# Two norms behind gated residuals: their shift seeded into PSUM by TensorE, residual and sums of squares by halves of the columns, shift vectors summed as columns

## The chip, the cores and the metric

The kernel runs on one core of a Trainium2 chip. The metric is the device time of one execution in microseconds. The kernel before took 904.48 us (median of three runs, 904.3 to 905.38).

## The reference, cut to what matters

The input is 256 tokens of 1024 features in float32. A first block (attention, then a squared-ReLU MLP) is followed by two modulated layers. Each modulated layer makes six vectors of 1024 from a condition `c`, and uses them as shift, scale and gate:

```python
def ada_modulation(c, ada_w, ada_b):
    m = jax.nn.silu(c) @ ada_w + ada_b
    return jnp.split(m, N_MOD, axis=-1)          # sh_m, sc_m, g_m, sh_f, sc_f, g_f

def modulate(h, shift, scale):
    return h * (1.0 + scale[:, None, :]) + shift[:, None, :]

def odd_layer(x, c, ...):
    h = modulate(rms_norm_2(x, mix_norm), sh_m, sc_m)
    ...                                          # qkv, stick-breaking attention
    x = x + g_m[:, None, :] * (o @ w_out)
    hf = modulate(rms_norm_2(x, ffn_norm), sh_f, sc_f)
    return x + g_f[:, None, :] * swiglu(hf, ffn_w_gate, ffn_w_up, ffn_w_down)
```

The layer before it (`even_layer`) has the same form, with a convolution and a linear recurrence in place of attention. The change touches the two norms of the odd layer: the one in front of its qkv projection (behind layer 0's swiglu and its gate `g_f`), and the one in front of its swiglu (behind the output projection and the gate `g_m`).

## The kernel before, in words

The 256 tokens lie as two tiles of 128 on the partitions (tile 0, tile 1), with 1024 columns each. `x` is the residual, `xn` the normed rows. TensorE needs the normed rows transposed, so they are transposed in blocks of 128 x 128 into two PSUM banks per tile (`norm_T`), and are copied from there to `aT_hi` by ScalarE (`norm_hi`), with the rest after rounding in `aT_lo` by VectorE (`norm_lo`). Every product is made of three matmuls in the rounded type fp32r: hi x hi, hi x lo, lo x hi.

Weights stream through four slots of 128 x 1024 elements ("parts"). SyncE's queue loads part v into `w_raw`, ScalarE rounds it to `w_hi` (L691), VectorE makes `w_lo` (L1104), TensorE uses both and then counts `w_used`. ScalarE may not write a slot before TensorE has counted `w_used` for the part three before it; SyncE may not load one before VectorE has made the `w_lo` of the part four before it. A unit is two parts. All engines run their instructions strictly in the order written; in the attention-like stages this order is written out by hand in the strings `ATT_STEPS`, `LRU_STEPS` and `STICK_STEPS` (H: round a part to `w_hi`, L: its `w_lo`, U and P: products of a unit or a part, and so on). Each engine picks from the string the steps that are its own.

The order of stages that matters here: the LRU stage (layer 0, mixer), ending with the output projection, units U10 to U13; the entry of layer 0's swiglu (`entry(U_SG0)`, norm number k = 3); the swiglu loop; the entry of the qkv stage (`entry(U_QKV2)`, k = 4); the stick stage (layer 1, attention, and its output projection P24 to P30); the entry of layer 1's swiglu (`entry(U_SG1)`, k = 5); the swiglu loop and the last residual. The three entries are called the **first**, the **second** and the **third entry** below.

An entry works like this. TensorE ends the products of the stage before, tile 0 first (`tile0_done`), then tile 1 (`w_used`). VectorE multiplies tile 0 by the gate and adds it to `x` (`gate`, `add_gated`: L1223, L1227), ScalarE squares and sums the row (L701), GpSimd makes 1/sqrt of the mean (L613, L614), VectorE has meanwhile multiplied `x` by the gain (`norm_scale`, L1118) and then makes `xn * rstd + shift` in two halves of 512 columns (`norm_rows`, L1127). TensorE transposes (L1831), ScalarE copies the banks (L744), and products with the first unit's weights follow (L1876, in `entry`): six groups for tile 0 with `aT_hi`, of which the last two want `w_hi` of parts 2 and 3 of that entry, then two with `aT_lo`, then the transposes of tile 1, and so on. At the second and third entry ScalarE's program rounds parts 2 and 3 in between (`norm`, L719 to L738). Norms k = 1 and 2 already work by halves of the columns and take their 1/sqrt from ScalarE's Ln and Exp (`half_square`, `half_rstd`: L714, L708, L710).

The modulation vectors are accumulated by VectorE as products per partition (`ada`), so each is spread over 128 partitions and has still to be summed over them. `ada_sums` (L2034 to L2042) does that with a matmul of `ones` (128 x 128, float32) and 512 columns of the vector, which gives the sum on every partition; ScalarE copies it back from PSUM (`ada_parts`, L747 to L755). Twelve such matmuls belong to layer 1: four at the first entry, four behind layer 0's swiglu at the second, four in front of layer 1's swiglu at the third. `ada_gain` (L1313) makes (1 + scale) x gain of the sum.

ScalarE's functions come in table sets; Silu, Sigmoid and Ln with Exp are in different ones, Copy and Square in all. Before, one set is loaded at the start of the stick stage (L1044), another in front of its Sigmoids (L1059).

## Time and profile before

| what | value |
|---|---|
| median of three runs | 904.48 us |
| the profiled execution's own time | 904.1 us |
| its span in the trace | 901.9 us |
| TensorE busy | 890.9 us (99%), 5057 matmuls |
| VectorE busy | 691.2 us (77%) |
| ScalarE busy | 486.3 us (54%) |
| granted TensorE clock, mean | 0.999 |
| chain that ended last | TensorE 94%, VectorE 2%, ScalarE 2%, DMA 1%, issue 1% |

The profile is one execution; its own time is that of the span and 2.2 us around it. A timeline row gives the start in us from the span's start, the length in us, the engine (PE is TensorE, PEld its loads of the stationary operand, DVE VectorE, ACT ScalarE, POOL GpSimd), the line, the operation, out and in with shapes, the count, and in brackets how long the engine was idle before and what ended that. The lengths of matmuls include their pipeline, so starts, not ends, tell how fast they follow one another. A float32 matmul stands in the trace as two matmuls with a load each; an fp32r matmul and a transpose as one.

### The profile page before, as it was taken

What the parts mean: (1) busy time and instruction counts of PE and PEld (TensorE: products, weight loads), DVE (VectorE), ACT (ScalarE), POOL (GpSimd) and SP (SyncE); (2) the same over time, 40 slices, a digit from 0 to 9 for tenths busy, and PEclk for the clock granted to TensorE, in tenths of its full rate; (3) what the DMA queues carried; (4) which work ended last, traced back from release to release, by engine and by line L of the source; (5) the groups of instructions that cost most, each with busy time, mean ns of one, the idle gap of its engine ahead of it and who ended that gap; (6) DMA issues with size and microseconds to landing.
All of it is one profiled execution on the core that took longest, in us unless ns stands there. A gap on an engine that the chain in (4) does not pass through costs nothing.

```text
span 901.9 us, 13646 instructions
## 1 busy us (share of the span) xinstructions
PE 890.9 (99%) x5057; PEld 762.2 (85%) x5057; DVE 691.2 (77%) x719; ACT 486.3 (54%) x650; POOL 29.4 (3%) x52
## 2 busy tenths in 40 slices
PE   8999999999999999999999999999999999999998
PEld 5998879999999799879888888878777888888886
DVE  4698978988888885976888888687797775555655
ACT  5545574444445657755454455455674465545542
POOL 4000100000000000012000000010000100000000
PEclk9999999999999999999999999999999999999999
DMA  6989586999998385645988888626434366656561
GB/s 217 339 273 341 177 292 215 356 362 328 321 329 311 107 269 162 213 139 171 370 304 315 321 302 286 190 90 217 139 117 139 107 209 198 189 186 186 187 188 68
DMA packets 117093, 208.08 MB, mean 231 GB/s; under 512 B 7236, under 2 KB 81068, under 8 KB 111928
## 3 DMA queue, kind: packets, MB, share of 16 engines
q1 hardware_dynamic: 116566, 205.31, 67.5%
q10 hardware_dynamic: 290, 2.10, 0.7%
q8 instruction: 30, 0.49, 0.2%
q14 instruction: 15, 0.12, 0.0%
q0 software_dynamic: 192, 0.05, 0.0%
HBM read 206.39 MB, written 1.05 MB: 230 GB/s over the span
## 4 chain that ended last, share of the span: by engine, by line
PE 94%; DVE 2%; ACT 2%; DMA 1%; issue 1%; SPq 0%; DVEq 0%; ACTq 0%
PE tp L1858 8%; PE ub L1858 8%; PE acc L1763 7%; PE acc L1764 7%; PE acc L1766 7%; PE acc L1711 5%; PE acc L1713 5%; PE acc L1712 5%; PE tp L1859 4%; PE ub L1859 4%; PE acc L1876 4%; PE tp L1876 4%; PE ub L1847 3%; PE ub L1846 3%; PE ub L1845 3%; PE acc L1845 2%
## 5 line engine op out<-in xcount | busy, mean ns | idle before, releaser
L1104 DVE TENSOR_TENSOR w_lo<-w_raw,w_hi 128x1024 fp32r<-128x1024 f32 x288 | 348.6, 1221 | 117.3 <-ACT w_hi L691 116.7
L691 ACT ACTIVATE w_hi<-w_raw 128x1024 fp32r<-128x1024 f32 x288 | 302.2, 1058 | 245.2 <-PE acc L1766 72.4
L1858 PE MATMUL tp<-aT,w_hi 128*128 128x512 f32 x320 | 114.1, 399 | 0.0
L1858 PE MATMUL ub<-aT,w_hi 128*128 128x512 f32 x320 | 113.8, 398 | 0.0
L1763 PE MATMUL acc<-w_hi,hT_hi 128*128 128x512 f32 x288 | 112.8, 392 | 0.1
L1764 PE MATMUL acc<-w_lo,hT_hi 128*128 128x512 f32 x288 | 112.2, 390 | 0.0
L1766 PE MATMUL acc<-w_hi,hT_lo 128*128 128x512 f32 x272 | 106.1, 390 | 0.0
L1859 PE MATMUL tp<-aT,w_lo 128*128 128x256 f32 x320 | 89.9, 281 | 0.0
L1859 PE MATMUL ub<-aT,w_lo 128*128 128x256 f32 x320 | 89.8, 281 | 0.0
L1858 PEld LDWEIGHTS tp<-aT,w_hi 128*128 128x128 f32 x320 | 60.1, 188 | 14.9
L1858 PEld LDWEIGHTS ub<-aT,w_hi 128*128 128x128 f32 x320 | 60.1, 188 | 14.6
L1845 PE MATMUL ub<-aT,w_hi 128*128 128x256 f32 x256 | 72.5, 283 | 0.0
L1846 PE MATMUL ub<-aT,w_hi 128*128 128x256 f32 x256 | 72.4, 283 | 0.0
L1847 PE MATMUL ub<-aT,w_lo 128*128 128x256 f32 x256 | 72.4, 283 | 0.0
L1711 PE MATMUL acc<-w_hi,aT 128*128 128x512 f32 x168 | 67.5, 402 | 0.2 <-DVE aT L1112 0.2
L1713 PE MATMUL acc<-w_hi,aT 128*128 128x512 f32 x168 | 65.5, 390 | 0.0
L1712 PE MATMUL acc<-w_lo,aT 128*128 128x512 f32 x168 | 65.5, 390 | 0.0
L1763 PEld LDWEIGHTS acc<-w_hi,hT_hi 128*128 128x128 f32 x288 | 54.1, 188 | 11.6 <-issue 0.3
L1764 PEld LDWEIGHTS acc<-w_lo,hT_hi 128*128 128x128 f32 x288 | 54.1, 188 | 10.5
L1859 PEld LDWEIGHTS ub<-aT,w_lo 128*128 128x128 f32 x320 | 60.4, 189 | 0.7
L1766 PEld LDWEIGHTS acc<-w_hi,hT_lo 128*128 128x128 f32 x272 | 51.1, 188 | 11.3
L1859 PEld LDWEIGHTS tp<-aT,w_lo 128*128 128x128 f32 x320 | 60.4, 189 | 0.0
(274 smaller groups left out, 1524.2 us busy)
## 6 DMA issues: line engine op xcount, KB each, us to landing
ada_raw<-in_l_ada_w SPq DMA_DIRECT2D x24, 1024.0 KB, 6.2
w_raw<-in_l_ffn_w_gate SPq DMA_DIRECT2D x44, 512.0 KB, 4.5
w_raw<-in_l_ffn_w_up SPq DMA_DIRECT2D x44, 512.0 KB, 3.9
w_raw<-in_l_ffn_w_down SPq DMA_DIRECT2D x44, 512.0 KB, 3.4
w_raw<-in_w_up SPq DMA_DIRECT2D x32, 512.0 KB, 4.4
w_raw<-in_w_down SPq DMA_DIRECT2D x32, 512.0 KB, 5.1
scratch<-in_l_ada_w SPq DMA_DIRECT2D x14, 1024.0 KB, 7.3
w_raw<-in_attn_w_qkv SPq DMA_DIRECT2D x24, 512.0 KB, 6.2
```

Of the source, the lines that this page charges most:

```text
L691: act.activation(w_hi[:, v % SLOTS, :], w_raw[:, v % SLOTS, :], ACT.Copy).then_inc(hi_done, 1)
L1104: dve.tensor_tensor(w_lo[:, n, :], w_raw[:, n, :], w_hi[:, n, :].bitcast(F32), ALU.subtract).then_inc(lo_done, 1)
L1711: pe.matmul(outp, op_hi[:, k + n, q], w_hi[:, s, c], start=start and n == 0, stop=False)
L1712: pe.matmul(outp, op_hi[:, k + n, q], w_lo[:, s, c], start=False, stop=False)
L1713: last = pe.matmul(outp, op_lo[:, k + n, q], w_hi[:, s, c], start=False, stop=stop and n == 1)
L1763: pe.matmul(outp, operand[0][:, k, q], w_hi[:, s, c], start=start, stop=False)
L1764: last = pe.matmul(outp, operand[0][:, k, q], w_lo[:, s, c], start=False, stop=False)
L1766: last = pe.matmul(outp, operand[1][:, k, q], w_hi[:, s, c], start=False, stop=stop)
L1845: pe.matmul(outp, wh, aT_hi[:, b, :], start=b == 0, stop=False)
L1846: pe.matmul(outp, wh, aT_lo[:, b, :], start=False, stop=False)
L1858: pe.matmul(banks[f], w_hi[:, v % SLOTS, c], aT[:, :, b, :], start=b == 0, stop=False)
L1859: last = pe.matmul(banks[f][:, 0:TOK], w_lo[:, v % SLOTS, c], aT_hi[:, b, :], start=False, stop=b == KB - 1)
```

## The change

The shift of norms k = 4 and 5 is no longer added by VectorE. Its vector (spread over 128 partitions as products) is summed with eight float32 matmuls of one column each, `shift` as the stationary operand, which gives it as 8 columns of 128 (`shift_sums`); ScalarE copies them twice into a zeroed tile of 40 columns (`shift_copy`), TensorE transposes that (`shift_T`), ScalarE rounds the 40 rows (`shift_hi`) and VectorE puts the rounding's rest into rows 32 to 39 (`shift_rest`). In front of the transposes of such a norm TensorE writes the shift into both banks with one fp32r matmul each (K = 40, 512 columns, `pick` chooses the row), and the transposes accumulate onto it (`seeded_T`). So VectorE needs only `x * rstd * gain`, without a `norm_scale` before it.

For the first shift the step N0 (sums) stands in the LRU stage between W1 and U12 and V0 (transpose, rounding, rest) between U12 and H14; for the second, X0 and Y0 stand in the stick stage.

Both norms work by halves of the columns with `half_square` and `half_rstd`; GpSimd only adds eps. The four `ada_sums` of shifts fall away. The gate's two sums (GATE_M) are made in fp32r from a rounded copy and its rest: ScalarE and VectorE make these at the end of layer 0's swiglu, between rounding the last parts. So layer 1 has two `ada_sums` at the first entry, two and the two `gate_sums` (in front of tile 1's transposes) at the second, two at the third, of which one in front of tile 1's transposes. The table load of the stick stage's start stands now at the end of layer 0's swiglu, and there is a new one behind the last Sigmoid of the stick stage. Layer 1's second gain is made in the stick stage (step I0), not behind the second entry. The third entry makes the `w_lo` of its second part earlier.

The diff, cut to its core:

```diff
-STICK_STEPS = steps("""... T0 B0 H9 L9 P6 H10 L10 P7 Q1 R1 N1 H11 L11 P8 H12 L12
+STICK_STEPS = steps("""... T0 B0 H9 L9 X0 P6 H10 L10 P7 Q1 R1 N1 H11 L11 Y0 I0 P8 H12 L12
-    U11 H13 L13 I0 W1 U12 H14 U13""")
-ADA_ORDER = tuple(range(12)), (0, 1, 2, 3, 4, 5, 8, 9, 6, 7, 10, 11)
+    U11 H13 L13 I0 W1 N0 U12 V0 H14 U13""")
+ADA_ORDER = tuple(range(12)), (2, 3, 8, 9, 4, 5, 10, 11)
+        gate_hi, gate_lo = (aT[:, n, :, P:TOK] for n in range(2))
+        def shift_banks(n):
+            return (ub, tp)[n][:, 0, 0:KB], (ub, tp)[n][0:SH_K, 1, 0:P]
...
 # ScalarE
+            def shift_copy(n):
+                act.wait_ge(sh_sum, n + 1)
+                act.wait_ge(pick_done, 3)
+                both = sh_cols.rearrange("p (r b) -> p r b", b=KB)[:, 0:SH_K // KB:LO_ROW // KB, :]
+                act.activation(both, shift_banks(n)[0].unsqueeze(1).broadcast_to([P, 2, KB]), ACT.Copy).then_inc(sh_copied, 1)
+            def shift_hi(n):
+                act.wait_ge(sh_T, n + 1)
+                act.activation(sh_rows[:, :], shift_banks(n)[1], ACT.Copy).then_inc(sh_hi, 1)
...
+                if layer == 0:
+                    act.preload_act_table_set("natural_log_exp_and_others")
+                    act.wait_ge(ada_used, 40)
+                    act.activation(gate_hi, GATE_M.rearrange("p (b n) -> p b n", n=P), ACT.Copy).then_inc(ada_hi, 1)
                 split_hi(u + 3 * NJ_SG)
+            def tile_rows(k, t):
+                n = 2 * (k - 4) + t
+                act.wait_ge(x_half, 5 + n)
+                half_square(t, 0, x[:, t, 0:CH], sq_half)
+                act.wait_ge(x_ready, 2 * k - 1 + t)
+                half_square(t, 1, x[:, t, CH:D], sq_done)
+                half_rstd(t, 1, 9 + n)
+            def qkv_norm(u):
+                tile_rows(4, 0)
+                split_part(2 * u + 2)
+                norm_hi(4, 0)
+                split_part(2 * u + 3)
+                tile_rows(4, 1)
+                ada_parts(1, 2, 3)
+                norm_hi(4, 1)
+                ada_parts(1, 3, 6)
+            def last_norm(u):
+                tile_rows(5, 0)
+                norm_hi(5, 0)
+                split_part(2 * u + 2)
+                tile_rows(5, 1)
+                split_part(2 * u + 3)
+                norm_hi(5, 1)
+                ada_parts(1, 6, 8)
...
+                    if n == 7:
+                        act.preload_act_table_set("natural_log_exp_and_others")
...
 # VectorE
+            def shift_rest(n):
+                dve.wait_ge(sh_hi, n + 1)
+                dve.tensor_tensor(sh_rows[LO_ROW:SH_K, :], shift_banks(n)[1][LO_ROW:SH_K, :],
+                                  sh_rows[LO_ROW:SH_K, :].bitcast(F32), ALU.subtract).then_inc(sh_lo, 1)
+            def qkv_norm(u):
+                dve.wait_ge(half_done, 3)
+                gated(0, gate_ffn, 0).then_inc(x_half, 1)
+                dve.wait_ge(tile0_done, 4)
+                gated(0, gate_ffn, 1).then_inc(x_ready, 1)
+                dve.wait_ge(half_done, 4)
+                gated(1, gate_ffn, 0).then_inc(x_half, 1)
+                norm_rows(0, G_M, None)
+                dve.wait_ge(w_used, parts_to(u))
+                gated(1, gate_ffn, 1).then_inc(x_ready, 1)
                 norm_lo(0, 0)
                 norm_lo(0, 1)
+                norm_rows(1, G_M, None)
...
-                split_lo(u + 3 * NJ_SG)
+                if layer == 0:
+                    split_part(2 * U_QKV2)
+                    dve.wait_ge(ada_hi, 1)
+                    dve.tensor_tensor(gate_lo, GATE_M.rearrange("p (b n) -> p b n", n=P), gate_hi.bitcast(F32),
+                                      ALU.subtract).then_inc(ada_lo, 1)
+                    split_part(2 * U_QKV2 + 1)
...
 # TensorE
+            def seeded_T(k, t):
+                banks = norm_banks(k, t)
+                if t == 0:
+                    pe.wait_ge(sh_lo, k - 3)
+                for g, bank in enumerate(banks):
...
+                    pe.matmul(bank.rearrange("p (b n) -> p b n", n=P), sh_rows[:, :],
+                              pick[:, 4 * g:4 * g + 4].unsqueeze(2).broadcast_to([SH_K, 4, P]), start=True, stop=False)
+                for g, bank in enumerate(banks):
+                    pe.wait_ge(xn_done, 4 * k + 2 * t + g + 1)
+                    for b in range(4):
+                        last = pe.matmul(bank[:, b * P:(b + 1) * P], xn[:, t, (4 * g + b) * P:(4 * g + b + 1) * P],
+                                         ident[:, :], start=False, stop=b == 3, is_transpose=True)
+            def shift_sums(n, shift):
+                for b in range(KB):
+                    last = pe.matmul(shift_banks(n)[0][:, b:b + 1], shift[:, b * P:(b + 1) * P], ones[:, 0:1],
+                                     start=b == 0, stop=b == KB - 1)
+            def shift_T(n):
+                pe.wait_ge(sh_copied, n + 1)
+                pe.transpose(shift_banks(n)[1], sh_cols[:, :], ident[:, :]).then_inc(sh_T, 1)
+            def gate_sums():
+                pe.wait_ge(ada_lo, 1)
+                pe.wait_ge(x_ready, 8)
+                for m in (16, 17):
+                    b = slice(4 * (m - 16), 4 * (m - 15))
+                    out = sum_bank(m).rearrange("p (b n) -> p b n", n=P)
+                    pe.matmul(out, ones_r[:, :], gate_hi[:, b, :], start=True, stop=False)
+                    pe.matmul(out, ones_r[:, :], gate_lo[:, b, :], start=False, stop=True).then_inc(ada_sum, 1)
...
-            ada_sums(1, 0, 4)
+            ada_sums(1, 0, 2)
...
-            ada_sums(1, 4, 8)
-            entry(U_QKV2, (acc[:, 0, :], acc[:, 1, :]), ada_parts=20)
+            ada_sums(1, 2, 4)
+            entry(U_QKV2, (acc[:, 0, :], acc[:, 1, :]), before_T1=gate_sums)
...
-            ada_sums(1, 8, 12)
+            ada_sums(1, 6, 7)
```

## Rows read from the trace of the kernel before

**Rows 1.** The page, part 1: engine, busy us, share of the span, instructions.

```profile
PE 890.9 (99%) x5057; PEld 762.2 (85%) x5057; DVE 691.2 (77%) x719; ACT 486.3 (54%) x650; POOL 29.4 (3%) x52
```

**Rows 2.** The chain that ended last, in order of time: start, length, what.

```profile
371.96 1.72 PE tp L2041 x4
...
399.07 1.98 PE ub L2041 x4
...
591.29 1.98 PE ub L2041 x4
...
594.39 2.54 PE acc L1876 x10
...
599.47 7.28 PE acc L1876 x32
...
711.53 4.20 PE tp L1876 x32
715.74 0.87 PE acc L1831 x8
```

**Rows 3.** Loads of the stationary operand at L2165 and L1960: min/median/max ns.

```profile
L2165 PEld LDWEIGHTS acc<-ada_raw,scratch x32: 132/137/137, 668.2 to 675.3; 128*64 128x64 f32 x32
...
L1960 PEld LDWEIGHTS ub<-scratch x16: 187/192/192, 47.6 to 90.0; 128*128 128x128 f32 x16
```

**Rows 4.** Timeline of the loads of five small transposes in the attention stage.

```profile
35.66 0.32 PEld L1992 LDWEIGHTS ub<-ident,scratch 11*128 11x128 f32 x4
35.90 0.14 PEld L1993 LDWEIGHTS ub<-ident,scratch 8*128 8x128 f32 x1
```

**Rows 5.** Timeline, from the LRU stage's unit U12 to the first entry.

```profile
389.81 1.98 PE L1736 MATMUL acc<-w_hi,aT 128*128 128x512 f32 x8
390.98 2.01 ACT L691 ACTIVATE w_hi<-w_raw 128x1024 fp32r<-128x1024 f32 x2 [4.04 <-PE acc L1736]
...
392.14 1.23 DVE L1104 TENSOR_TENSOR w_lo<-w_raw,w_hi 128x1024 fp32r<-128x1024 f32 x1 [4.00 <-ACT w_hi L691]
...
393.28 0.68 DVE L1223 TENSOR_TENSOR xn<-acc,mod 128x512 f32<-128x512 f32 x1
...
394.61 0.68 DVE L1223 TENSOR_TENSOR xn<-acc,mod 128x512 f32<-128x512 f32 x1
...
400.77 0.48 PEld L1831 LDWEIGHTS acc<-ident,xn 128*128 128x128 f32 x4 [0.55 <-DVE xn L1127]
```

**Rows 6.** Timeline of ScalarE around one table load of the LRU stage.

```profile
354.96 1.28 ACT L980 ACT_TABLE_LOAD   x1
356.26 1.71 ACT L980 ACTIVATE xn<-scratch,lam 128x256 f32<-128x256 f32 x4
```

**Rows 7.** Timeline, from the end of layer 0's swiglu to the second entry.

```profile
579.92 0.63 ACT L999 ACTIVATE hT_hi<-scratch 128x512 fp32r<-128x512 f32 x1 [0.53 <-DVE scratch L1612]
...
583.41 1.06 ACT L691 ACTIVATE w_hi<-w_raw 128x1024 fp32r<-128x1024 f32 x1 [1.66 <-PE acc L1766]
...
586.14 1.23 DVE L1223 TENSOR_TENSOR xn<-acc,gate_ffn 128x1024 f32<-128x1024 f32 x1 [0.41 <-PE acc L1782]
...
588.60 1.88 PE L2041 MATMUL ub<-mod,ones 128*128 128x512 f32 x4
...
591.17 1.41 DVE L1127 SCALAR_TENSOR_TENSOR xn<-xn,rstd,mod 128x512 f32<-128x512 f32 x2
```

**Rows 8.** Timeline of ScalarE in norm k = 2, which works by halves.

```profile
303.11 0.63 ACT L714 ACTIVATE scratch<-x 128x512 f32<-128x512 f32 x1
...
304.19 0.20 ACT L710 ACTIVATE rstd<-log_var 128x1 f32<-128x1 f32 x1
```

**Rows 9.** Timeline at the third entry.

```profile
704.91 0.69 DVE L1227 TENSOR_TENSOR x<-x,xn 128x512 f32<-128x512 f32 x1
...
706.72 3.69 PE L2041 MATMUL ub<-mod,ones 128*128 128x512 f32 x8
```

**Rows 10.** Windows: us, then busy (count) by engine, granted clock, DMA share, GB/s.

```profile
588.76:594.39 5.63, 4.58 (x16) 2.03 (x15) 5.53 (x6) 3.61 (x7) 0.75 (x2) 1.00 0.02 8
```

More of the change, by code:

```diff
@@ L89 @@
     G15 U14 H16 L16 U15""")
-STICK_STEPS = steps("""H4 L4 H5 L5 Q0 R0 N0 H6 L6 H7 L7 P4 H8 L8 P5 T0 B0 H9 L9 P6 H10 L10 P7 Q1 R1 N1 H11 L11 P8 H12 L12
+STICK_STEPS = steps("""H4 L4 H5 L5 Q0 R0 N0 H6 L6 H7 L7 P4 H8 L8 P5 T0 B0 H9 L9 X0 P6 H10 L10 P7 Q1 R1 N1 H11 L11 Y0 I0 P8 H12 L12
     P9 T1 B1 H13 L13 P10 H14 L14 P11 Q2 R2 N2 H15 L15 P12 H16 L16 P13 T2 B2 H17 L17 P14 H18 L18 P15 Q3 R3 N3 H19
@@ L174, in block_program @@
         mod_next = ada_raw[:, 1, :]
+        SH_M, G_M, GATE_M, SH_F, G_F = (mod[:, c * D:(c + 1) * D] for c in range(5))
         ada_slot = [ada_raw[:, 0, :], ada_raw[:, 2, :]] + [scratch[:, n * UNIT:(n + 1) * UNIT] for n in range(1, 5)]
@@ L290, in block_program @@
         ada_out = sem("ada_out")
+        ada_hi = sem("ada_hi")
+        ada_lo = sem("ada_lo")
+        sh_sum = sem("sh_sum")
+        sh_copied = sem("sh_copied")
+        sh_T = sem("sh_T")
+        sh_hi = sem("sh_hi")
+        sh_lo = sem("sh_lo")
+        pick_done = sem("pick_done")
         ada_gain_done = sem("ada_gain_done")
@@ L991, in _ @@
                     act.activation(aT_hi[:, 0:LB, :], conv_a, ACT.Copy).then_inc(y_hi, 1)
-            norm(U_SG0, 1, (0, 0, 2, 4))
+            norm(U_SG0, 1, (0, 0, 2, 2))
             def swiglu(layer):
@@ L1081, in _ @@
                     act.activation(hi, bank, ACT.Copy).then_inc(so_hi, 1)
-            norm(U_SG1, 1, (8, 8, 10, 12))
+            last_norm(U_SG1)
             swiglu(1)
@@ L1242, in gated_out @@
                 gated(1, g_mod, 1).then_inc(x_ready, 1)
-            def gated_norm(n, u_end, g_mod, g, shift):
-                dve.wait_ge(tile0_done, n + 1)
-                gated(0, g_mod).then_inc(x_ready, 1)
-                dve.wait_ge(x_ready, 2 * n + 1)
-                norm_scale(0, g)
-                dve.wait_ge(w_used, parts_to(u_end))
-                gate(1, g_mod)
-                norm_rows(0, g, shift)
-                add_gated(1).then_inc(x_ready, 1)
-                dve.wait_ge(x_ready, 2 * n + 2)
-                norm_scale(1, g)
+            def shift_rest(n):
+                dve.wait_ge(sh_hi, n + 1)
+                dve.tensor_tensor(sh_rows[LO_ROW:SH_K, :], shift_banks(n)[1][LO_ROW:SH_K, :],
+                                  sh_rows[LO_ROW:SH_K, :].bitcast(F32), ALU.subtract).then_inc(sh_lo, 1)
@@ L1257, in gated_norm, with last_norm @@
                 norm_lo(0, 1)
-                norm_rows(1, g, shift)
-                split_part(2 * u_end + 2)
+                norm_rows(1, G_M, None)
+                split_part(2 * u + 2)
                 norm_lo(1, 0)
                 norm_lo(1, 1)
-                split_part(2 * u_end + 3)
+                split_part(2 * u + 3)
+            def last_norm(u):
+                split_part(2 * u)
+                dve.wait_ge(w_used, parts_to(u - 1))
+                gated(0, GATE_M, 0).then_inc(x_half, 1)
+                split_part(2 * u + 1)
+                dve.wait_ge(tile0_done, 5)
+                gated(0, GATE_M, 1).then_inc(x_ready, 1)
+                gated(1, GATE_M, 0).then_inc(x_half, 1)
+                norm_rows(0, G_F, None)
+                dve.wait_ge(w_used, parts_to(u))
+                gated(1, GATE_M, 1).then_inc(x_ready, 1)
+                norm_lo(0, 0)
+                norm_lo(0, 1)
+                norm_rows(1, G_F, None)
+                split_part(2 * u + 2)
+                norm_lo(1, 0)
+                split_part(2 * u + 3)
+                norm_lo(1, 1)
@@ L1319, in ada_gain @@
                 dve.scalar_tensor_tensor(part, part, 1.0, gain[:, g % 4, :], ALU.add, ALU.mult).then_inc(ada_gain_done, 1)
-            SH_M, G_M, GATE_M, SH_F, G_F = (mod[:, c * D:(c + 1) * D] for c in range(5))
             def copy_chunk(u, bank, ct):
@@ L1527, in _ @@
                     ada(2, 4, 0, n, 23, src=ada_last, dst=mod_next)
+                elif step == "V":
+                    shift_rest(0)
                 elif step == "I":
@@ L1685, in _ @@
                     stick_mask(n)
+                elif step == "Y":
+                    shift_rest(1)
+                elif step == "I":
+                    ada_gain(1, 4, 16)
                 elif step == "A":
```

78 lines of the change are left out of this document (62 added, 16 removed).

## The prediction

> **What bounds the kernel.** The page's first part comes first: TensorE is busy 99% of the span [rows 1], so time comes from two places only: TensorE work added or taken away where nothing waits, and the hand-over at the entries. The chain of waits shows the second. At the second entry it goes through two sums that waited for ScalarE's copies (591.29) before the transposes and the first product at 594.39; at the third it has tile 0's products from 711.53, tile 1's transposes from 715.74 [rows 2]. At the first entry TensorE's load stood 0.55 us for VectorE's norm at 400.77 [rows 5]. So I read each entry as a race of three queues, and the stretches between as a sum of TensorE work.
>
> **Prices.** A float32 sum of 512 columns costs 0.86 us: four of the chain's matmuls, two for each sum, take 1.72 us [rows 2]. An fp32r matmul of 512 columns costs 0.227 us (7.28 us / 32), a product of 256 columns at the third entry 0.13 us (4.20 us / 32), eight transposes 0.87 us [rows 2].
>
> **The one-column sums** are in no row. Each is two matmuls with a load of 128 columns, so 16 loads per shift. Loads of 64 columns last 137 ns, of 128 columns 187 to 192 ns [rows 3]: 51 ns for 64 columns, hence about 105 ns per 128 columns if loads follow one another, 16 x 0.105 = **1.7 us**. The low end is the small transposes' loads, which start every 60 ns (35.66 to 35.90 for four) [rows 4]: 1.0 us. The high end is a whole load each time, 16 x 0.187 = 3.0 us. I take 1.7, since float32 loads of 128 rows are nearest. One shift thus costs as much as the two sums it replaces (1.72 us), but it stands in stretches where TensorE is full, while the removed ones stood partly in waits.
>
> **First entry and LRU stage.** N0 puts 1.7 us in front of U12; TensorE waits for nothing there, so all of it is on the path: +1.7. V0 is worse than its size. ScalarE's next rounding (H14) started at 390.98, as soon as U12's half-way matmul, in the group that began at 389.81, had freed a slot, and had idled 4.04 us; VectorE's `w_lo` followed at 392.14 [rows 5]. Now ScalarE stands in V0 until TensorE has ended U12 and done the transpose: U12 ends at about 391.6 in the old times (389.81 + 8 x 0.227), the transpose and its way out add 0.3, ScalarE's small copy 0.25. H14 starts near 392.15 instead of 390.98: 1.15 us later. Queued behind it is the `w_lo` and, behind that in VectorE's order, every gated half of the residual. They follow without a gap (pairs every 1.33 us, 393.28 and 394.61) up to the norm, for which the transposes waited [rows 5]. So +1.15, bounded by 0.5 (if the transpose is seen at once) and 1.6. The two sums that leave this entry gave nothing to the path: behind them TensorE waited for VectorE anyway, so taking away 1.72 us of work gives back 0 to 0.1. `shift_rest` hides in VectorE's wait.
>
> **Stick stage.** X0: +1.7, on a full TensorE. The two transposes of 40 columns, one per shift, cost 0.1 each (0.87/8); V0's is hidden, as VectorE's chain ends last there; Y0's is not: +0.1. Behind X0, ScalarE's copy (0.2) waits until the sums are done; the next rounding has to wait for its weights there. Y0 and I0 put 1.4 us on VectorE between L11 and L12; part 12 is needed three parts later (at 3 us each), and the load behind L12 goes out 1.4 us later with as much time to land. Both cost 0; without that cover I0 would cost 1.2. The new table load behind the last Sigmoid delays a rounding and a copy by half a us, whose users come more than 1 us later: 0.
>
> **Second entry.** Before: last products end near 588.7, tile 0's first product starts 594.39, tile 1's transposes end at 599.47 [rows 2, 7]. After, ScalarE ends `hT_hi` at 580.55 [rows 7], loads its table (1.28 us, the next instruction 0.02 us behind it [rows 6]) and copies the gate (1.06): the two roundings end at 583.9 and 584.85; the second started at 583.41 before [rows 7]. VectorE makes `w_lo` from 583.98, `gate_lo` (1.2), the second `w_lo`, and is done at 587.5; it takes up half 0 of tile 0 at 587.45, 1.3 us later than it took up the whole tile before (586.14) [rows 7]. Two pairs of 1.33 us end at 590.15. The half's square, Ln and Exp take 1.28 us (303.11 to 304.39) [rows 8]: 1/sqrt at 591.45. `norm_rows` has no scale in front of it: halves at 592.2 and 592.9, against 591.9 and 592.6 [rows 7]. Before, though, the transposes waited for the second pair of sums (591.29 + 1.98) [rows 2]; now only two sums and two seeds stand in front and end at 590.8. Transposes of half 0 from 592.3; from their start to the first product it was 1.1 us (593.27 to 594.39) [rows 2] and is 1.2 with part 2 rounded in front of the copy: 593.5: **0.9 us earlier**. From there TensorE is full: 16 products 3.6, `gate_sums` 0.9 (4 x 0.227), seeds 0.45, transposes 0.87, end 599.3 against 599.47. Effect: **-0.15**, from -0.9 (the start's gain kept) to +0.6 (the second tile's norm, which ends at 598.3 by the same steps, misses TensorE at 598.4). What the gate's split costs in waits and what its sums save about cancel.
>
> *The Trainium skill ("ScalarE: Activation LUTs", section "What ACT_TABLE_LOAD costs") adds a drain of some 1.38 us to each such switch. The row shows none; by the page this entry would come 1.4 us later and the sum would be +6.4.*
>
> **Third entry.** Before: last product out at 706.7, four sums (706.72, 3.69), product at 711.53. VectorE's add ends at 705.6 [rows 9], ScalarE's 1/sqrt now at 706.9, `norm_rows` at 707.7 and 708.4 without waiting for the shift's sums; TensorE does one sum (0.86) and two seeds (0.45) until 708.0, transposes until 708.9, first product 709.15: **2.4 us earlier**. But tile 0's sixth group wants `w_hi` of part 3. ScalarE's order is now: copies (709.6), part 2 (710.6), tile 1's squares with 1/sqrt (1.9, 712.45), part 3 (713.4). TensorE asks for it at 709.15 + 20 x 0.13 = 711.75 and waits 1.65 us. Then 12 products 1.55, the sum moved in front of tile 1 0.86, seeds 0.45, transposes 0.87: end near 717.1, against 715.74 + 0.87 = 716.6. Effect: **+0.5**, between -1.5 (no stall) and +1.2.
>
> **The sum.** 1.7 + 1.15 + 1.7 + 0.1 - 0.15 + 0.5 = +5.0. Against the profiled execution's 904.1 us that is 909.1; the median lies 0.4 higher, so **909.5**. About 0.2% (1.8 us) is what a measurement of this kernel can tell from no change. As pure TensorE work the change adds 3.4 + 0.9 + 1.8 (seeds) + 0.2 and removes 6 x 0.86 = 5.2: +1.1. The rest is the wait at V0 and the removed sums' cover.
>
> **Rivals.**
> - *The earlier starts are kept (not slower).* Place: the second and third entry. If ScalarE has part 3 in time (before 711.75) and the backlog behind the second entry's start is absorbed, the starts' 0.9 and 2.4 us stay: 5.0 - 0.35 - 3.3 = +1.35, 905.9. For it: at both entries VectorE's norm was what it waited on. Against: ScalarE's order. With one-column sums at 60 ns per load this gives about 904.5. Chance 0.13.
> - *Cheap one-column sums* (1.0 us each): +3.6, 908.1. Part of my forecast's range. *Dear ones* (3.0 each): +7.6, 912.1, decided by whether a load hides behind a one-column matmul. Chance 0.08.
> - *The clock.* The first entry leaves TensorE without work for some 3 us: its first two sums had ended before 399.07, where the second pair began [rows 2], and the transposes come at 400.77 + 1.15 [rows 5]. Before, the stretch 588.76 to 594.39 had 4.58 us busy of 5.63 and clock 1.00 [rows 10], so no row shows a gap as long in full work. If the clock fell to 1.2 GHz for tile 0's products, 4.2 us, would take twice that: +9.2, 913.7. Chance 0.06. The Trainium skill ("TensorE: Matmul & The Clock Gate", section "Why this matters for your kernels") warns that idle gaps between bursts bring the half clock back; no row here shows one.
> - *It does not do what it says.* The "half" at the second entry is taken up later than the whole tile was, which is in the sum.
>
> **Chances.** Forecast 0.71 (with cheap sums), earlier starts kept 0.13, dear sums 0.08, clock 0.06, something faster that I don't see 0.02. Of the forecast about a twentieth falls under +1.8. Faster 0.04, within 0.2% 0.14, slower 0.82. The range reaches from 906.0 (just above the kept starts) to 912.1 (dear sums); the clock lies outside.
>
> **What would show it.** Right: eight one-column sums with 16 loads over about 1.7 us; ScalarE's first rounding behind V0 later by 1.15 us against TensorE's U12, and the first entry's transposes waiting for VectorE; at the second entry VectorE's first gated half starting behind two `w_lo` and `gate_lo`; at the third a wait of TensorE for L691 of 1.65 us in tile 0's products. Wrong: a first entry with no longer wait than before, sums under 1 us, or a third entry whose tile 1 transposes come over 1 us earlier after its last product.

## The result: 912.2 us, 0.85% slower

The changed kernel takes 912.2 us, the median of 4 runs (911.73 to 912.69), against 904.39 us (4 runs) of the kernel before: ratio 1.0085, interval 1.0068 to 1.0103. The profiled execution took 912.0 us with a span of 910.0 us, against 904.1 and 901.9. It is slower, as forecast, and sits just above 912.1, the end of the range.

The page of the kernel after, its first part, in the order of [rows 1]:

```profile
PE 894.6 (98%) x5091; PEld 766.6 (84%) x5091; DVE 688.2 (76%) x722; ACT 490.6 (54%) x671; POOL 26.8 (3%) x49
```

TensorE is 3.7 us busier than in [rows 1] and its share has fallen: 8.1 us of span are 3.7 of busy time and 4.4 of waiting. Some 1.1 of the 3.7 is not more work but the same work at a lower clock, as the first entry shows below. The chain that ended last, start, length and what, says where:

```profile
386.22 1.68 PE ub L2176 x16
...
404.35 1.02 PE acc L1970 x4
405.37 5.02 PE tp L2015 x32
...
411.26 7.68 PE tp L2015 x64
...
603.07 1.02 PE tp L1956 x8
604.09 7.30 PE acc L2015 x32
...
617.71 1.68 PE tp L2176 x16
...
720.48 1.67 PE tp L2015 x12
...
723.63 1.03 PE acc L1956 x8
724.66 7.67 PE tp L2015 x64
```

Each entry ends with a run of products behind tile 1's transposes. Like events of the two traces stand against each other as follows (us from each span's start; the shift is after less before), so each stage's cost is a difference of two shifts. The first pair is the work just ahead of N0, the last the gated residual that ends the kernel.

| event | before | after | shift | the stage's own |
|---|---|---|---|---|
| work ahead of N0 | 384.59 | 384.50 | -0.09 | |
| first entry's end | 407.32 | 411.26 | +3.94 | +4.0 |
| second entry's end | 599.47 | 604.09 | +4.62 | +0.7 |
| third entry's first sum (stick stage done) | 706.72 | 713.30 | +6.58 | +2.0 |
| third entry's end | 716.61 | 724.66 | +8.05 | +1.5 |
| last residual | 893.51 | 901.56 | +8.05 | 0 |

**First entry.** The timelines of ScalarE and TensorE after the change, around V0 and up to the products (start, length, engine, line, what, idle before and releaser):

```profile
391.71 1.76 PE L1851 MATMUL acc<-w_hi,aT 128*128 128x512 f32 x7
393.30 0.27 PE L2182 MATMUL ub<-ident,sh_cols 128*40 128x128 f32 x1
...
398.90 1.88 PE L2201 MATMUL ub<-ada_raw,ones 128*128 128x512 f32 x4
403.69 1.68 PE L1970 MATMUL acc<-ident,xn 128*128 128x128 f32 x8 [2.91 <-DVE xn L1209]
```

```profile
393.61 0.27 ACT L834 ACTIVATE sh_rows<-ub 40x128 fp32r<-40x128 f32 x1 [5.50 <-PE ub L2182]
393.79 1.99 ACT L715 ACTIVATE w_hi<-w_raw 128x1024 fp32r<-128x1024 f32 x2
```

The group of eight at L1851 starts at 391.48 (the record of its first matmul is missing, so the row has seven), ScalarE's rounding at 393.79: 2.31 us apart, where [rows 5] have 1.17. So V0 cost 1.14. Behind it everything is later by N0 and V0 together, and TensorE stands idle for 2.91 us. Then a thing happens that the kernel before does not show. Windows of the kernel after (us, busy time by engine, granted clock, DMA share, GB/s):

```profile
401.00:403.69 2.69, 0.00 (x1) 0.00 (x1) 2.62 (x5) 2.10 (x5) 0.77 (x2) 1.00 0.00 0
403.69:405.00 1.31, 1.30 (x8) 1.03 (x8) 1.31 (x2) 1.06 (x3) 0.76 (x1) 0.81 0.00 0
405.00:408.19 3.19, 3.19 (x18) 3.16 (x16) 3.16 (x5) 2.49 (x3) 1.89 (x2) 0.54 0.49 143
408.19:410.40 2.21, 2.21 (x21) 2.21 (x20) 2.15 (x3) 0.00 (x0) 1.13 (x1) 1.00 0.10 35
```

The granted clock is at its lower level (1.2 GHz) for most of the second and third window, from the second half of the transposes on, and is back at 2.4 GHz in the last. It falls when TensorE works again, not in the idle stretch. The transposes' second half took 1.02 us and the 32 products 5.02, against 0.66 and 4.31 in an execution in which the clock stayed up (the experiment with the table load, below): 1.1 us.

**Second entry.** Tile 0's first half of columns is gated at 591.28, and the first product comes at 597.52, 3.13 us later than in [rows 2], with a shift of 3.94 at the last entry's end: 0.8 us of the earlier start are real. What follows, on a TensorE that is never free, takes more than they gave:

```profile
596.18 1.32 PE L1956 MATMUL tp<-ident,xn 128*128 128x128 f32 x8 [1.12 <-DVE xn L1209]
597.52 1.23 PE L2015 MATMUL acc<-w_hi,aT 128*128 128x512 f32 x4
...
601.34 0.40 PE L2191 MATMUL acc<-aT,ones_r 128*128 128x512 f32 x1
...
602.37 0.70 PE L1951 MATMUL tp<-pick,sh_rows 40*128 40x512 f32 x2
603.00 1.09 PE L1956 MATMUL tp<-ident,xn 128*128 128x128 f32 x8
```

From the first product to the end (604.09) it is 6.57 us, against 5.08 in [rows 2]: 1.03 of gate sums (601.34 to 602.37), 0.63 of seeds and 0.2 more for the transposes (1.09 us) are new, while the 16 products take 3.82 (597.52 to 601.34) where 5.08 less the transposes' 0.87 made 4.2. In front of this stretch TensorE waits 1.12 us for VectorE's norm, where before it waited for ScalarE's copies. ScalarE's order is the reason:

```profile
584.53 1.28 ACT L1082 ACT_TABLE_LOAD   x1
585.82 1.06 ACT L1084 ACTIVATE aT<-mod 128x1024 fp32r<-128x1024 f32 x1
586.79 1.99 ACT L715 ACTIVATE w_hi<-w_raw 128x1024 fp32r<-128x1024 f32 x2
```

Its table load puts the roundings, `w_lo`, and with them VectorE's first gated half back, so that the norm's rows came late.

**Third entry.** The first product comes at 716.23, 1.9 us earlier against the entry's first sum (713.30) than before. Then the forecast stall:

```profile
718.24 0.64 PE L2015 MATMUL tp<-w_hi,aT 128*128 128x256 f32 x4
720.48 1.67 PE L2015 MATMUL tp<-w_hi,aT 128*128 128x256 f32 x12 [1.60 <-ACT w_hi L715]
```

### The profile page after: what moved, and what is told of

Read it like the earlier page. It is cut to its first block, busy times and chain, and to the rows that moved or that the text cites. A ratio compares the mean times of both kernels' runs of the same rounds, so it can differ in the third digit from the quotient of the medians.

```text
span 910.0 us, 13738 instructions
## 1 busy us (share of the span) xinstructions
PE 894.6 (98%) x5091; PEld 766.6 (84%) x5091; DVE 688.2 (76%) x722; ACT 490.6 (54%) x671; POOL 26.8 (3%) x49
## 3 DMA queue, kind: packets, MB, share of 16 engines
HBM read 206.39 MB, written 1.05 MB: 228 GB/s over the span
## 4 chain that ended last, share of the span: by engine, by line
PE 92%; DVE 3%; ACT 2%; DMA 1%; issue 1%; SPq 0%; DVEq 0%; ACTq 0%
PE tp L1997 8%; PE ub L1997 8%; PE acc L1878 7%; PE acc L1879 7%; PE acc L1881 7%; PE acc L1826 5%; PE acc L1828 5%; PE acc L1827 5%; PE tp L1998 4%; PE ub L1998 4%; PE tp L2015 4%; PE acc L2015 3%; PE ub L1986 3%; PE ub L1985 3%; PE ub L1984 3%; PE acc L1984 2%
```

## Experiments

All times are medians; each group of kernels ran on one chip beside the kernel before. That kernel's own median was 904.39 beside the change, 904.29 in the group of experiments 1 to 4, 903.82 in that of 6 to 9 and 904.62 in that of 5 and 10, so a difference of two medians from different groups is uncertain by some tenths of a us, up to 0.8. Within a profile nothing of this kind enters. The profiled executions differ among themselves by up to 1.5 us at the LRU stage's sums near 372 (371.96 in [rows 2]), ahead of all that the change touches, so a stage is always measured from its own first event.

### 1. The first shift's rounding a unit earlier

```diff
-    U11 H13 L13 I0 W1 N0 U12 V0 H14 U13
+    N0 U11 H13 L13 V0 I0 W1 U12 H14 U13
```

> The first shift's one-column sums stand in front of U11 instead of U12, and V0 (transpose, rounding, rest) behind H13 and L13 instead of in front of H14. Theory A (ScalarE's wait in V0 delays VectorE's chain by 1.14 us, and the gap that this leaves on TensorE lets the clock fall to 1.2 GHz for the first entry, 1.15 us more): ScalarE's first rounding behind U12 starts 1.2 us after the group of eight matmuls with the low part begins (after the change 2.3), the first entry's granted clock is back near 1.00, and the time is 912.2 - 2.3 = 909.9. Rival B (the wait is covered, or the slow products come from the order of the entry itself): at most 0.3 us less, 911.9 or more. Middle case, the wait goes but the clock falls all the same: 911.0.

Measured: 911.57 us (911.14 to 911.93), ratio 1.0078 (1.0061 to 1.0095). ScalarE's rounding is back where it was against TensorE's group, and the first entry is healed:

```profile
393.19 2.01 ACT L715 ACTIVATE w_hi<-w_raw 128x1024 fp32r<-128x1024 f32 x2 [4.04 <-PE acc L1851]
...
392.02 1.98 PE L1851 MATMUL acc<-w_hi,aT 128*128 128x512 f32 x8
```

1.17 us between the two, as in [rows 5]. From that group's start to the first entry's end it is 17.63 us, against 19.78 in the change and 17.51 before: V0's 1.14 and the clock's 1.07 are gone (0.2 of it is lost again ahead of that group). But the whole kernel won only 0.6. This chain of waits of the same execution and the windows beside it show where 1.6 went:

```profile
595.90 5.57 PE acc L2015 x16
```

```profile
592.00:595.90 3.90, 2.75 (x12) 1.13 (x10) 3.81 (x7) 2.77 (x6) 0.49 (x1) 1.00 0.22 86
595.90:598.00 2.10, 2.10 (x6) 1.64 (x7) 1.79 (x3) 2.08 (x5) 0.00 (x0) 0.59 0.00 0
```

The clock fell at the second entry instead, behind the same wait of 1.1 us that the change has there; the 16 products took 5.57 us against 3.99. The mean granted clock of all four runs is 0.998, as it is in all four of the change; in the kernel before it is 0.999 or 1.000 in all runs but one of the 49 beside these experiments. A mean of 0.998 or less goes with a fall inside the work, in every one of the 13 profiled executions of this document: seven have both, six (0.999 or 1.000) neither. Where in the kernel it fell is known only for these.

### 2. Something to do in the first entry's gap

Three float32 products of 512 columns, whose result nobody reads, behind the first entry's sums.

```diff
             ada_sums(1, 0, 2)
+            for n in range(3):
+                pe.matmul(tp[:, n % 2, :], ones[:, :], mod_next[:, 0:CH], start=True, stop=True)
```

> V0 stays where the change puts it; behind the first entry's two sums TensorE does three more float32 matmuls of 512 columns (2.6 us) into banks that the first product overwrites; their result is never used. They end at about 403.2, before the norm's first half at 403.6. Theory A (clock): granted clock 1.00 from 403.7 to 411, tile 1's transposes end 1.15 us earlier, 911.05. Rival B (the entry's products are slow for another reason, such as a busy port or VectorE's late rest): the same 0.54 clock is not there to be healed, no gain or up to 0.2 us more, 912.2 to 912.4.

Measured: 911.67 us (911.43 to 912.25), ratio 1.0082 (1.0066 to 1.0099). The timeline of TensorE and the window of the products:

```profile
401.24 2.74 PE L2284 MATMUL tp<-ada_raw,ones 128*128 128x512 f32 x6
404.32 1.32 PE L1970 MATMUL acc<-ident,xn 128*128 128x128 f32 x8 [0.34 <-DVE xn L1209]
```

```profile
405.00:408.00 3.00, 2.98 (x23) 2.74 (x24) 2.97 (x4) 2.92 (x4) 2.80 (x2) 1.00 0.23 56
```

With 2.58 us more work on TensorE the kernel did not get slower, and the clock stayed up: the mean granted clock is 1.000 in three of four runs. So the gap's idle time costs nothing by itself, and with work in it the products kept their clock. From those sums near 372 to the third entry's end this execution is 1.04 us shorter than the change's (351.75 against 352.79), which is what the clock had cost. The medians show only 0.5 of it, from different groups, with ranges that overlap. The wait at the second entry is still there, as long as in experiment 1, and in three of the four runs the clock held all the same.

### 3. ScalarE's part 3 ahead of tile 1's squares

```diff
                 split_part(2 * u + 2)
-                tile_rows(5, 1)
                 split_part(2 * u + 3)
+                tile_rows(5, 1)
```

> At the third entry ScalarE rounds part 3 before tile 1's squares and 1/sqrt. Theory A (TensorE's 1.60 us wait is that order alone): the wait goes, tile 1's norm comes at 721.8 by ScalarE's queue (two roundings, then 1.9 us of squares and 1/sqrt, then 0.75 per half), and the transposes end at 722.7 instead of 724.66: 1.9 us less, 910.3. Rival B (the wait moves to tile 1's norm, which is now late by a rounding): under 0.6 us less, 911.6 or more.

Measured: 910.38 us (909.84 to 912.87), ratio 1.0075 (1.0058 to 1.0091). The chain at the third entry:

```profile
716.20 4.13 PE tp L2015 x32
720.33 0.86 PE ub L2201 x2
721.19 0.63 PE acc L1951 x2
721.82 1.02 PE acc L1956 x8
```

No wait is left among the products. From the entry's first sum to its end it is 9.56 us (713.28 to 722.84) against 11.36 in the change and 9.89 in [rows 2, 9]. So ScalarE's order was worth 1.8 us, and with it the third entry is 0.3 us faster than before. The clock fell in the first entry in this execution too.

### 4. The table load behind the gate copy and the roundings

```diff
-                    act.preload_act_table_set("natural_log_exp_and_others")
                     act.wait_ge(ada_used, 40)
                     act.activation(gate_hi, ...)
                 split_hi(u + 3 * NJ_SG)
+                if layer == 0:
+                    act.preload_act_table_set("natural_log_exp_and_others")
```

> At the end of layer 0's swiglu the table load stands behind the two roundings instead of in front of the gate's rounding. Theory A (VectorE's chain of w_lo, gate_lo, w_lo and gated halves sets the second entry): VectorE's first gated half starts at 590.0 instead of 591.28, the first product at 596.2 instead of 597.52, the transposes of tile 1 end 1.2 us earlier, 911.0. Rival B (TensorE's own work sets it, which begins with two sums and two seeds until 595.0): the start comes 1.1 us earlier, but the transposes of tile 1 wait for their norm, and under 0.4 us is left: 911.8 or more.

Measured: 910.81 us (910.54 to 911.05), ratio 1.0071 (1.0055 to 1.0088). ScalarE's timeline:

```profile
587.30 1.07 ACT L715 ACTIVATE w_hi<-w_raw 128x1024 fp32r<-128x1024 f32 x1 [0.96 <-PE acc L1882]
588.39 1.28 ACT L1086 ACT_TABLE_LOAD   x1
591.24 0.64 ACT L738 ACTIVATE scratch<-x 128x512 f32<-128x512 f32 x1 [1.57 <-DVE x L1310]
```

The load now lies in time in which ScalarE waits anyway. From its sums to its end the second entry takes 10.36 us (592.49 to 602.85) against 11.54 (592.55 to 604.09): 1.18 less. TensorE no longer waits for the norm, so the wait of 1.12 was about all that could be won. In this execution the first entry had its gap of 2.91 us as in the change, and the clock did not fall there: 32 products in 4.31 us. One idle stretch, two outcomes; in the other three runs of this kernel the mean clock is 0.997 or 0.998.

### 5. One product in place of eight

```diff
-                for b in range(KB):
-                    last = pe.matmul(shift_banks(n)[0][:, b:b + 1], shift[:, b * P:(b + 1) * P], ones[:, 0:1],
-                                     start=b == 0, stop=b == KB - 1)
+                last = pe.matmul(shift_banks(n)[0], shift[:, 0:P], ones[:, 0:KB], start=True, stop=True)
```

> In the change, one product of 8 columns takes the place of the eight one-column products of each shift; 7 of 8 column blocks of both shifts are left out of the sums, so the shifts added are not the reference's. My theory (the products lie on the path in both stages, 1.68 us each, and their loads set it): 14 of 16 loads gone in each, 1.47 us each, 912.2 - 2.9 = 909.3. Rival (the LRU stage's wait for the rounding is then longer, as VectorE and ScalarE are not ready sooner): 910.8.

Measured: 909.41 us (908.68 to 909.88), ratio 1.0052 (1.0037 to 1.0067). 2.8 us less than the change. In the profile it is 1.57 less from the sums near 372 to the first entry's end and 1.55 less in the stick stage, so all that the products take lies on the path, in both stages. The two matmuls, with a load each, that are left of the first shift's:

```profile
386.71 0.28 PE L2175 MATMUL ub<-ones,ada_raw 128*128 128x8 f32 x2
```

### 6. No seeds

```diff
-                    pe.matmul(bank.rearrange("p (b n) -> p b n", n=P), sh_rows[:, :],
-                              pick[...].broadcast_to([SH_K, 4, P]), start=True, stop=False)
...
-                                         ident[:, :], start=False, stop=b == 3, is_transpose=True)
+                                         ident[:, :], start=True, stop=True, is_transpose=True)
```

> The seeds (products of the shift's rows with pick) are left out, and the transposes start their banks themselves; the shift is so not added behind either of the two gated residuals, and the rest is as in the change. My theory (each pair of seeds costs 0.62 us where nothing covers it): the last entry loses its two pairs from the path, 1.2 us, and the second entry one pair, 0.6 (its other pair lies beside a wait): 912.2 - 1.9 = 910.3. Rival (in the waits for the norm's rows the seeds are covered, and the next wait takes their place): 911.5 to 912.2.

Measured: 910.75 us (910.45 to 912.28), ratio 1.0079 (1.0063 to 1.0094), so 1.5 less than the change, but only 0.9 less when each is taken against the kernel before beside it. In its profile the third entry takes 10.24 us (713.20 to 723.44), 1.12 less than the change: two pairs of seeds. At the second entry tile 0's pair was covered by the wait, which grew:

```profile
596.88 1.23 PE L1954 MATMUL tp<-ident,xn 128*128 128x128 f32 x8 [1.83 <-DVE xn L1209]
```

1.83 of idle time in place of 1.12: 0.7 of seeds had lain in it. The four pairs are 2.5 us of TensorE time (0.62 each); three of them lay on the path, 1.12 and 0.7 us by the profile. The fall at the first entry cost 0.2 us more in this execution than in the change's, so that the whole is 1.6.

### 7. The three places together

Experiments 1, 3 and 4 in one kernel.

> The rounding of the first shift a unit earlier, ScalarE's part 3 ahead of tile 1's squares in the last entry, and the table load behind the gate copy, all in one kernel. My theory (the places are independent and lie on the path): 0.6 + 1.8 + 1.2 to 1.4, so 908.3 to 908.7 us against 912.2 of the change. In the profile: first shift's rounding 1.17 us behind the sums' group as before the change, no TensorE wait for the norm's rows in the second entry, none for ScalarE's part in the last. Rival A (what one place gives is taken back at the next wait): 910 or more. Rival B (the first entry's clock falls in some executions and not in others, and the single kernels' medians are blurred by it): 907.2, as the earlier rounding alone is then worth 1.1 more.

Measured: 907.25 us (906.66 to 908.39), ratio 1.0037 (1.0024 to 1.0051). 4.95 less than the change, where the three alone won 0.6, 1.8 and 1.4. The mean clock is 0.999 or 1.000 in four of the five runs (the fifth is the slowest). The profiles, in which the clock can be seen, show how it adds up. Each number is how much shorter a stage is than in the change; "first" runs from the sums near 372 to the first entry's end, the others from one entry's end to the next.

| | first | second | third | sum |
|---|---|---|---|---|
| experiment 1 alone (clock fell at the second entry) | 1.95 | -1.57 | 0.01 | 0.39 |
| experiment 3 alone (clock fell at the first) | -0.10 | 0.03 | 1.80 | 1.73 |
| experiment 4 alone (clock held) | 1.05 | 1.19 | -0.02 | 2.22 |
| the three together (clock held) | 1.95 | 1.19 | 1.77 | 4.91 |

So the three places are independent, and what one of them wins is kept in full once the clock stays. By the median the rival that said 907.2 was right, and not my own theory of 908.3 at the least. Against the kernel before on the same chip it is 4.4 less than the change, between the two, so the profiles carry this and not the medians. TensorE still has idle time in front of the first entry's transposes:

```profile
402.69 1.32 PE L1971 MATMUL acc<-ident,xn 128*128 128x128 f32 x8 [1.95 <-DVE xn L1210]
```

### 8. The first shift summed in the gap

As 7, and N0 and V0 leave the LRU stage: the sums stand behind the first entry's sums, where TensorE waits for the norm.

```diff
-    N0 U11 H13 L13 V0 I0 W1 U12 H14 U13
+    U11 H13 L13 I0 W1 U12 H14 U13
...
             ada_sums(1, 0, 2)
+            pe.wait_ge(ada_used, 24)
+            shift_sums(0, mod_next[:, 0:D])
...
+            def first_shift():
+                pe.wait_ge(ada_out, 14)
+                shift_T(0)
...
-                entry(u, tp_banks, gated=True, before_T1=(lambda: ada_sums(1, 7, 8)) if layer else None)
+                entry(u, tp_banks, gated=True, before_T1=(lambda: ada_sums(1, 7, 8)) if layer else first_shift)
```

> As the last, and the first shift's 16 loads are moved out of the LRU stage into TensorE's idle 2.9 us ahead of the first entry's first tile (the transposes of sh_cols before tile 1's). My theory: the sums (1.68) and the rounding wait (1.14) leave the path, one small transpose (0.1 to 0.3) stays on it, and the gap shrinks below that at which the clock fell; against the change 1.68 + 1.14 - 0.2 + 1.8 + 1.3 = 5.7 less: 906.5, and 905.4 where the clock's 1.1 is also saved. Rival (the entry's own work for ScalarE and VectorE comes late, by the copy of 0.3, the rounding of 0.2 and the rest of 0.2 that now lie in it): up to 0.7 more, 907.2. If the path does not lead through TensorE in the LRU stage: as c1.

Measured: 906.16 us (904.95 to 906.47, 11 runs), ratio 1.0021 (1.0012 to 1.0030). In the profile, from the unit's products ahead of N0 to the first entry's end it is 30.10 us (378.31 to 408.41), against 32.07 (377.15 to 409.22) in experiment 7: 2.0 less. The median won only 1.1. The mean clock is 0.998 in 7 of 11 runs, where it was in 1 of 5: the gap is full, and yet the clock falls at least as often (five runs are too few to say more often). The profiled execution is one in which it held.

### 9. The second shift by transposes

As 8, and X0 makes 8 transposes of SH_F's blocks into the two banks; VectorE sums them along the row.

```diff
+                    if n:
+                        last = pe.transpose(tp[:, b // 4, (b % 4) * P:(b % 4 + 1) * P], shift[:, b * P:(b + 1) * P],
+                                            ident[:, :])
+                        continue
...
+                    dve.reduce_sum(sh_cols[:, 0:KB], tp[:, :, :].rearrange("p a (b n) -> p (a b) n", n=P),
+                                   AX.X).then_inc(sh_red, 1)
```

> As the last, and the second shift's columns are made by 8 transposes and a reduction on VectorE in place of the 8 one-column products. My theory (one-column float32 products load 16 times, 105 ns each; a transpose loads once, 60 ns): 8 x 0.06 = 0.5 us against 1.68, so 1.2 less than c2: 905.3 to 904.2. Rival (the small transposes end no sooner, their results being 128 columns wide; or the 1.1 us of VectorE for 1024 elements delays a chunk that TensorE waits for): as c2, or 0.5 above it.

Measured: 905.61 us (904.34 to 905.98, 11 runs), ratio 1.0014 (1.0005 to 1.0023). From the second entry's end to the third's it is 117.83 us (600.08 to 717.91) against 118.80, 1.0 less, of which the medians show 0.55. The eight transposes took 0.87 us, not the 0.5 that I had priced by small transposes' loads:

```profile
613.68 0.87 PE tp L2195 x8
```

### 10. Wide columns in the gap

As 9; the first shift's products have 64 equal columns instead of one, and the first of each is read.

```diff
-                    last = pe.matmul(shift_banks(n)[0][:, b:b + 1], shift[:, b * P:(b + 1) * P], ones[:, 0:1],
+                    last = pe.matmul(tp[:, 0, b * DENSE:(b + 1) * DENSE], shift[:, b * P:(b + 1) * P], ones[:, 0:DENSE],
```

> As the kernel with the second shift by transposes, but the first shift's 8 products, now just ahead of the first entry's norm, take 64 equal columns each in place of one. The loads set their rate (105 ns each), and 64 columns of the pace of the entry's 128-column tiles (137 ns) take some 70 ns, so the products should stay 1.7 to 1.9 us. My theory (the clock falls after thin work as after idle time, and denser columns hold it): profile with the clock at 1.00 through the first entry, mean clock 0.999 or 1.000 in most runs where the kernel with one column has 0.998 in 7 of 11, and 0.5 to 0.8 us less: 904.8 to 905.1. Rival (what is in the columns doesn't matter to the clock): 905.6, the same share of runs at 0.998. Rival (64 columns pace the products): 1.7 more.

> The kernel with the second shift by transposes once more, beside the last on the same chip: 905.6, with the mean clock at 0.998 in more than half of the runs.

Measured side by side on one chip: 905.18 us (904.31 to 905.99, 11 runs) with 64 columns, ratio 1.0003 (0.9994 to 1.0012); 905.74 (905.12 to 907.35, 11 runs) with one, ratio 1.0014 (1.0005 to 1.0023). The groups last equally long; first the timeline with 64 columns, then with one:

```profile
399.52 1.89 PE L2200 MATMUL tp<-ones,ada_raw 128*128 128x64 f32 x16
```

```profile
400.03 1.84 PE L2198 MATMUL tp<-ones,ada_raw 128*128 128x1 f32 x16
```

Then the windows of the entry's products behind them, of each kernel again in this order:

```profile
401.90:407.20 5.30, 5.22 (x41) 4.63 (x40) 5.27 (x8) 3.22 (x6) 2.77 (x3) 1.00 0.34 100
```

```profile
402.40:404.00 1.60, 1.52 (x10) 1.07 (x9) 1.60 (x3) 1.38 (x5) 1.35 (x2) 0.80 0.00 0
404.00:407.00 3.00, 3.00 (x16) 3.00 (x16) 2.97 (x5) 1.86 (x2) 1.31 (x1) 0.54 0.60 178
```

The mean clock is 0.999 or 1.000 in all 11 runs with 64 columns, and 0.998 in 9 of the 11 with one (in experiment 9, the same kernel, in 6 of 11). In the profiles the starts of the two groups and of the transposes behind them are 1.98 us apart in both. The forecast of 0.5 to 0.8 us less came to 0.56, with ranges that overlap; the share of runs with a low clock, 0 of 11 against 9 of 11, is the clearer sign. (The expectation speaks of tiles of 128 columns at 137 ns; the entry's products have 256 columns and take 135 ns, 4.31 us / 32.)

No version beats the kernel before. The best of them, with 64 columns, cannot be told from it.

## Why the prediction was right or wrong

The sign, the places and most of the mechanism were right; the size was 2.7 us short, because the clock fell, a rival with a chance of 0.06, and because two entries cost more than their terms.

- **First entry and LRU stage, one-column sums.** Forecast 1.7 for 16 loads; the chain has 1.68 at both places (105 ns for each load; the slope in the forecast's own rows, 51 ns for 64 columns, makes 102). Experiment 5, without 14 of the 16 in each, won 2.8 for the 2.94 that this makes. The two bounds, 60 ns and 187 ns per load, and their cheap and dear rivals, fall.
- **V0's wait.** Forecast 1.15, measured 1.14, and experiment 1 took it back.
- **The removed sums' cover.** Forecast no gain at the first entry, right: TensorE waited 2.91 us behind the two that were left. Filling the time with 2.58 us of dummy work cost nothing.
- **The clock.** The rival named the place and the cause that preceded it (a gap of some 3 us ahead of tile 0's products) and was right about the event, but not about its size, which it had as the products' doubling, +4.2. It was 1.1: the clock was back at 408, before tile 0's products had ended (410.4). A chance of 0.06 was too low, because no row of before showed such a gap with the clock kept, and I let "no row shows it" count against it. Experiment 2 is the test of the cause: with work in the gap the mean clock is 1.000 in three of four runs, without it in none of the change's four. The Trainium skill ("TensorE: Matmul & The Clock Gate", section "Why this matters for your kernels") warns of idle gaps; the traces agree at this entry in four of the five profiled executions that have this gap (experiment 4's is the fifth), and experiment 9, whose clock fell with no gap there, shows that it isn't idle time alone.
- **Stick stage.** Forecast 1.8, measured 1.96; the products are 1.7 of it and the small transpose some 0.1. What the last 0.1 is was not looked into.
- **Second entry.** Forecast -0.15, measured +0.67, a little outside its bounds. The start was right: gated half forecast for 591.39 by the shift (587.45 + 3.94) and seen at 591.28, first product forecast 0.9 earlier and seen 0.8 earlier. The step that failed is "from there TensorE is full: 16 products 3.6, gate sums 0.9, seeds 0.45, transposes 0.87": they took 3.82, 1.03, 0.63 and 1.09. I had priced each by a mean over a long run of one kind; the pair of seeds cost 0.62 for 0.45. Whether that comes from the change of kind or from the seeds' own form (40 rows, repeated columns) no run here tells. The table load was in the forecast's chain, at its right size; what the forecast did not ask was whether it had to stand there. Experiment 4 shows that its place alone is worth 1.18.
- **The table load.** The Trainium skill ("ScalarE: Activation LUTs", section "What ACT_TABLE_LOAD costs") adds a drain of some 1.38 us to the load. The trace again shows the load's 1.28 and the next instruction 0.01 us behind it, and the instruction ahead of it had ended 0.02 us before. That moving it won 1.18 tells nothing of the drain, as only the wait of 1.12 stood to be won.
- **Third entry.** The stall of 1.65 us for part 3 was 1.60, and experiment 3 took it away. Forecast +0.5, at most +1.2, measured +1.47: the start was 1.9 and not 2.4 us earlier (the sum and the seeds in front of it 0.96 and 0.62, for 0.86 and 0.45, and 1.35 from the first transpose to the first product, for 1.15), and tile 1's seeds and transposes are 0.62 and 1.10, for 0.45 and 0.87. Experiment 6 gives the seeds' share, 1.12 for two pairs, where the forecast had 0.9.
- **The sum.** 1.7 + 1.15 + 1.8 - 0.15 + 0.5 = 5.0, measured 1.67 + 1.14 + 1.96 + 0.67 + 1.47 + 1.1 of the clock = 8.0, against 8.1 between the two spans. Of the 3.0 that the forecast lacks, 1.1 is the clock, 1.0 the third entry and 0.8 the second. That the time lies beside the range's upper end is luck: that end stood for dear one-column sums, and these were not dear.
- **The rival of kept starts** fell for the reason it was given a low chance: ScalarE's order at the third entry, TensorE's fullness behind the start at the second. Experiment 7 shows what it would have needed: the same work in another order, 5 us less by the profile and still slower than before.

What stays open: which property of the work ahead decides on the clock in one execution and not in the next. The same kernel goes both ways (experiment 9), and I tried only two widths. Open too is whether the fall moved in experiment 1 because the first place was cured: experiment 2 cured it as well, kept the same wait at the second entry, and held its clock in three of four runs.

## What to carry to other kernels

Work moved onto the engine that is busy 98% of the time must replace work that was itself on the path; here the removed sums lay partly in waits, and their replacements did not. When an entry is split to start earlier, write down each other queue's order too: a rounding, a table load and two squares in the wrong place cost 1.1, 1.2 and 1.8 us, and none of them was the work that the change was about. And price a short group by its own kind of row, not by the mean of a long run.

## What the runs showed of the hardware

- A float32 product of a 128x128 block with one column costs 210 ns: two matmuls, 16 loads in 1.68 us for eight products. With 64 columns it costs as much (1.98 us from the group's start to the next in both), so 64 columns came for nothing.
- Eight transposes of 128x128 blocks took 0.87 us, half of that.
- Ahead of the first entry's transposes, with 2.91 us of idle time the run's mean clock was below 0.999 in 19 of 20 runs (the change and experiments 3 to 6), and in four of the five profiled ones the fall stands at this entry. With 1.95 us it was so in 1 of 5 (experiment 7), and in 4 of 4 where the second entry had a wait of 1.1 us besides (experiment 1). With float32 products of 512 columns in the gap: 1 of 4 (experiment 2). With no idle time but one-column products in its place: 7 of 11 (experiment 8) and 15 of 22 (the kernel of experiment 9), with 64-column products 0 of 11.
- A fall cost 1.0 to 1.6 us of profile time wherever it was seen. In the run times it shows as less: in the kernels of experiments 8 and 9 the median of the runs with a mean clock of 0.998 is 0.5 to 0.8 us above that of the others.
- Cured waits did not always show at once: in experiment 1's profiled execution 2.0 us were won up to the first entry's end and 1.6 lost to a fall at the second.
